# SSM group norms from column sums added on GpSimd, the skip product on ScalarE, another tile order, and no products for absent states

## The reference

```
zxbcdt = rms_norm(x, ln_g) @ in_w                 # z 2048, x 2048, B 512, C 512, dt 32 columns
xbc = silu(causal_dwconv(xbc, conv_w, conv_b))    # 4 taps; z is not convolved
dt = softplus(dt + dt_bias); a = dt * (-exp(a_log))
y = ssd_chunked(xs * dt, a, bm, cm)               # 4 chunks of 128 tokens, 4 groups of 8 heads
y = y + xs * d_skip[:, None]                      # the skip product
y = y.reshape(b, s, D_INNER) * silu(z)
y = rms_norm(y.reshape(b, s, 4, 512), norm_g)     # one norm for each group and token
return y @ out_w
# in ssd_chunked, for chunk c of group g:
#   y_diag = (C B^T, causal, times exp(decay)) x ; y_off = C state * exp(cumsum a) ; state = state * decay + B^T (decay x)
# the state before chunk 0 is zero
```

## Time and profile before

| what | us |
|---|---|
| time before, median of 3 runs | 2184.73 (2184.66 to 2185.71) |
| time of the profiled execution | 2181.98 |
| its span, first to last instruction | 2180.2 |
| PE busy in the span | 2117.6 (97%) |
| DVE busy | 1438.2 (66%) |
| ACT busy | 922.2 (42%) |
| POOL busy | 37.5 (2%) |

### The profile page before, as it was taken

How to read it: one execution, slowest core, us unless ns; L and a number is a source line. 1 busy time by engine, 2 the same in 40 slices (tenths; PEclk the granted TensorE clock), 3 DMA queues, 4 the chain that set the end, 5 groups by cost and what they waited for, 6 DMA issues and landing times.

```text
span 2180.2 us, 26967 instructions
## 1 busy us (share of the span) xinstructions
PE 2117.6 (97%) x10340; PEld 1677.1 (77%) x10340; DVE 1438.2 (66%) x2089; ACT 922.2 (42%) x1522; POOL 37.5 (2%) x100
## 2 busy tenths in 40 slices
PE   9999998899999999999899999999999999999998
PEld 7777776788888887777678888787777777767686
DVE  6687898777777345656577777447577657455664
ACT  5565655334444224444454444224343232344531
POOL 0000000000000000111000000000000000000000
PEclk9999999999999999999999999999999999999999
DMA  4321221222222333111132222333222224111132
GB/s 171 110 68 59 68 68 41 66 97 96 96 97 83 96 100 117 59 59 49 34 102 96 97 96 83 97 95 98 78 78 68 72 73 155 49 41 47 44 111 77
DMA packets 55072, 179.46 MB, mean 82 GB/s; under 512 B 6159, under 2 KB 7311, under 8 KB 54840
## 3 DMA queue, kind: packets, MB, share of 16 engines
q1 hardware_dynamic: 51264, 167.79, 23.8%
q10 hardware_dynamic: 3704, 10.30, 1.4%
HBM read 175.95 MB, written 4.74 MB: 83 GB/s over the span
## 4 chain that ended last, share of the span: by engine, by line
PE 76%; DVE 3%; ACT 1%; issue 0%; DMA 0%; DVEq 0%; ACTq 0%
PE bankpair L286 22%; PE bankpair L290 21%; PE bankpair L287 21%; PE bankpair L1445 1%; PE bankpair L699 1%; PE bankpair L1478 1%; PE bankpair L1459 1%; PE bankpair L719 1%; PE bankpair L1294 1%; PE bankpair L1306 1%; PE bankpair L709 1%; PE bankpair L664 1%; PE bankpair L1308 0%; PE bankpair L1392 0%; PE bankpair L674 0%
## 5 line engine op out<-in xcount | busy, mean ns | idle before, releaser
L286 PE MATMUL bankpair<-scaled_in_high,weights_high 128*128 128x512 f32 x1856 | 748.8, 403 | 5.0 <-DVE padded_rows L1747 2.2
L287 PE MATMUL bankpair<-scaled_in_low,weights_high 128*128 128x512 f32 x1856 | 728.0, 392 | 0.0
L310 ACT ACTIVATE weights_high<-weight_ring 128x1024 fp32r<-128x1024 f32 (+3 forms) x344 | 334.0, 972 | 314.1 <-DMA weight_ring<-down_dram 155.2
L290 PE MATMUL bankpair<-scaled_in_high,weights_low 128*128 128x512 f32 x1856 | 465.1, 389 | 0.0
L286 PEld LDWEIGHTS bankpair<-scaled_in_high,weights_high 128*128 128x128 f32 x1856 | 350.9, 189 | 89.9 <-issue 7.1
L321 DVE TENSOR_TENSOR weights_low<-weight_ring,weights_high 128x1024 fp32r<-128x1024 f32 (+3 forms) x344 | 383.8, 1125 | 54.5 <-ACT weights_high L310 45.0
L287 PEld LDWEIGHTS bankpair<-scaled_in_low,weights_high 128*128 128x128 f32 x1856 | 351.0, 189 | 76.4 <-issue 5.7
L290 PEld LDWEIGHTS bankpair<-scaled_in_high,weights_low 128*128 128x128 f32 x1856 | 348.6, 188 | 72.8
L286 PE MATMUL bankpair<-gated_high,weights_high 128*128 128x512 f32 x448 | 178.3, 398 | 4.6 <-DVE gated_low L2362 3.9
L287 PE MATMUL bankpair<-gated_low,weights_high 128*128 128x512 f32 x384 | 152.3, 397 | 0.0
L561 DVE SCALAR_TENSOR_TENSOR conv_rows<-padded_rows,params,conv_rows 128x512 f32<-128x512 f32 x176 | 131.8, 749 | 7.0 <-ACT conv_rows L530 3.8
(11 more groups left out here) (363 smaller groups left out, 2462.6 us busy)
## 6 DMA issues: line engine op xcount, KB each, us to landing
weight_ring<-up_dram SPq DMA_DIRECT2D x88, 512.0 KB, 3.6
weight_ring<-w_in_dram SPq DMA_DIRECT2D x70, 512.0 KB, 3.7
weight_ring<-in_w_dram SPq DMA_DIRECT2D x40, 512.0 KB, 3.7
weight_ring<-down_dram SPq DMA_DIRECT2D x32, 384.0 KB, 3.0
weight_ring<-kvq_dram SPq DMA_DIRECT2D x24, 512.0 KB, 3.7
weight_ring<-down_dram SPq DMA_DIRECT2D x32, 320.0 KB, 2.9
weight_ring<-out_a_dram SPq DMA_DIRECT2D x8, 512.0 KB, 3.7
weight_ring<-out_b_dram SPq DMA_DIRECT2D x8, 512.0 KB, 3.6
```

The source lines that it names most:

```text
L286: nc.tensor.matmul(bank, WH[:, high_slot, cell], high, start=(k == 0), stop=False)
L287: nc.tensor.matmul(bank, WH[:, high_slot, cell], low, start=False, stop=False)
L290: mm = nc.tensor.matmul(bank, WL[:, slot, cell], high, start=False, stop=(c == last_k))
L310: nc.scalar.activation(WH[:, (PART0[name] + k) % SLOTS, 0:n], RAW[:, b % SLOTS, 0:n], ACT.Copy).then_inc(high_ready, 1)
```

## The change

The mixer is rewritten in these places:

- Tile order within a group: B, C, x, z, where it was z, x, B, C. `FILL` becomes 2, 2, 3, 3. So chunk 0 is filled with B and C of the next group, chunk 1 with two tiles of x, chunk 2 with two of x and one of z, chunk 3 with three of z.
- Sums of squares: GpSimd adds the four squares of a unit to one (two instructions), and PE makes one product of it with a column of ones, which leaves a column of 128 sums. Root and reciprocal are taken of 128x4 elements, and PE spreads the four columns over the partitions with four transposes (`spread_root`) into bank 5. `group_norm` reads bank 5 and runs in chunk 3 of the next group (chunk 2 in the last group), after that unit's first tile.
- Since the sums of chunk 0 would overwrite a column that ACT has yet to read, PE waits for `gstd_ready` (ACT's root of the group before) ahead of the head of chunk 1 in groups 1 to 3.
- The skip product moves from DVE (one 128x512 instruction) to ACT (four of 128x128).
- In chunk 0, where the state is absent, ACT's `ECS` exponentials and DVE's two instructions on them are left out.
- One `split_low` in each unit comes before the wait for the exponentials.
- `ZS` is waited for by DVE's gating instead of by PE's head. The first `DTC` step on DVE comes ahead of `rows(0, 0)`.
- Three semaphores of the last norm of the program become one, with the same waits.

```diff
+        NORM_AT = {1: 3, 2: 3, 3: 2}
+        def exps_before(u):
+            return u - (u + NT - 1) // NT
+        def norms_before(u):
+            return sum(NT * g + NORM_AT[g] < u for g in NORM_AT)
+        def xb_row(j):
+            return GT + j if j < 2 else j - 2
-        FILL = [3, 2, 3, 2]
+        FILL = [2, 2, 3, 3]
+        CONVS = GT + 2
...
             def unit_sums(u):
-                pe.wait_ge(gsq_ready, u + 1)
-                for k in range(GT):
-                    mm = nc.tensor.matmul(BANK[4][:, 2 * P:3 * P], ONES[:, :], YSQ[:, k, :], start=(k == 0), stop=(k == GT - 1))
-                mm.then_inc(usum_done, 1)
+                pe.wait_ge(sq_added, 2 * u + 2)
+                at = 2 * P + u % NT
+                nc.tensor.matmul(BANK[4][:, at:at + 1], YSQ[:, 0, :], ONES[:, 0:1], start=True, stop=True).then_inc(usum_done, 1)
+
+            def spread_root(g, u):
+                pe.wait_ge(d_ready, u + 1)
+                pe.wait_ge(ginv_ready, g + 1)
+                for c in range(NT):
+                    mm = nc.tensor.transpose(BANK[5][:, c * P:(c + 1) * P], GINV[:, c:c + 1].to_broadcast([P, P]), IDENT)
+                mm.then_inc(gspread, 1)
...
                     if u >= 1:
                         pe.wait_ge(d_ready, u)
-                        pe.wait_ge(e_ready, 2 * u)
-                    if u >= 2:
-                        pe.wait_ge(gs_read, u - 1)
+                        pe.wait_ge(b_ready, u)
+                    if exps_before(u):
+                        pe.wait_ge(e_ready, exps_before(u))
+                    if c == 1 and g:
+                        pe.wait_ge(gstd_ready, g)
+                    if norms_before(u):
+                        pe.wait_ge(yn_ready, GT * norms_before(u))
...
-                            pe.wait_ge(row_used, GROUP_TILES * g + GT + j + 1)
+                            pe.wait_ge(row_used, GROUP_TILES * g + 2 + j + 1)
                         nc.tensor.transpose(BANK[5][:, j * P:(j + 1) * P], xb[:, j, tok], IDENT)
-                    if c == 0:
-                        pe.wait_ge(row_used, GROUP_TILES * (g + 1))
...
                             in_tile(g + 1, j)
+                            if g >= 1 and c == NORM_AT[g] and j == sum(FILL[:c]):
+                                spread_root(g - 1, u)
...
             for cells in (range(0, GT), range(GT, 2 * GT)):
                 for j in range(2):
                     gemm_tile(pe, "out_b", 0, j, lambda k: y_parts(k, j == 0), cells)
+                    if j == 0 and cells[0] == 0:
+                        spread_root(SSM_G - 1, UNITS - 1)
...
             def group_rms(g):
-                act.wait_ge(gs_read, NT * (g + 1))
-                nc.scalar.activation(STD[:, :], GSS, ACT.Sqrt, bias=EPSC[:, 0:1], scale=1.0 / (GT * P)).then_inc(gstd_ready, 1)
+                act.wait_ge(usum_done, NT * (g + 1))
+                if g:
+                    act.wait_ge(ginv_ready, g)
+                nc.scalar.activation(GROOT, BANK[4][:, 2 * P:2 * P + NT], ACT.Sqrt, bias=EPSC[:, 0:1],
+                                     scale=1.0 / (GT * P)).then_inc(gstd_ready, 1)
...
+                    for j in range(GT):
+                        skip = nc.scalar.activation(TMPY[:, j, :], XSB[g % 2][:, j, c * P:(c + 1) * P], ACT.Identity,
+                                                    scale=par("ssm_d", GT * g + j))
+                    skip.then_inc(skip_ready, 1)
...
                     act.wait_ge(yb_ready, u + 1)
+                    if u:
+                        act.wait_ge(usum_done, u)
                     nc.scalar.activation(YSQ, YB[:, GT * g:GT * (g + 1), c * P:(c + 1) * P], ACT.Square).then_inc(gsq_ready, 1)
                     if c == 0 and g >= 1:
                         group_rms(g - 1)
                         exp_tables(ahead)
-            square_sums(UNITS - 1)
+            nc.scalar.preload_act_table_set("sqrt_and_others")
             group_rms(SSM_G - 1)
...
+            for u in range(UNITS):
+                pool.wait_ge(gsq_ready, u + 1)
+                if u:
+                    pool.wait_ge(usum_done, u)
+                nc.gpsimd.tensor_tensor(YSQ[:, 0:2, :], YSQ[:, 0:2, :], YSQ[:, 2:4, :], ALU.add).then_inc(sq_added, 1)
+                pool.wait_ge(sq_added, 2 * u + 1)
+                nc.gpsimd.tensor_tensor(YSQ[:, 0, :], YSQ[:, 0, :], YSQ[:, 1, :], ALU.add).then_inc(sq_added, 1)
...
             def group_norm(g):
-                dve.wait_ge(gstd_ready, g + 1)
-                rs.step(nc.vector.reciprocal(RSG[:, :], STD[:, :]))
+                dve.wait_ge(gspread, g + 1)
...
-                    step.step(nc.vector.tensor_copy(etot, ecs[:, :, P - 1]))
-                    step.step(nc.vector.tensor_tensor(ecs, ecs, xb[:, GT + 1, tok].unsqueeze(1).to_broadcast([P, SSM_HG, P]),
-                                                      ALU.mult))
+                    if c:
+                        step.step(nc.vector.tensor_copy(etot, ecs[:, :, P - 1]))
+                        step.step(nc.vector.tensor_tensor(ecs, ecs, xb[:, GT + 1, tok].unsqueeze(1).to_broadcast([P, SSM_HG, P]),
+                                                          ALU.mult))
+                    if g + 1 < SSM_G:
+                        split_low(dve, BASE["in_w"] + GROUP_TILES * (g + 1) + sum(FILL[:c]) + 2)
...
-                    step.step(nc.vector.tensor_tensor(TMPY, xb[:, 0:GT, tok],
-                                                      par("ssm_d", GT * g, GT).unsqueeze(2).to_broadcast([P, GT, P]), ALU.mult))
+                    dve.wait_ge(skip_ready, u + 1)
                     dve.wait_ge(y_done, u + 1)
                     yr.step(nc.vector.tensor_tensor(TMPY, TMPY, BANK[6][:, :].rearrange("p (j t) -> p j t", t=P), ALU.add))
+                    if c == 0:
+                        dve.wait_ge(row_used, GROUP_TILES * (g + 1))
...
-                    if c == 0 and g >= 1:
-                        group_norm(g - 1)
+                    if c == 1 and g >= 1:
+                        group_inverse(g - 1)
```

94 lines of the change are left out of this document (53 added, 41 removed).

## The result

The changed kernel takes **2160.64 us** (median; 2157.72 to 2162.02 in 4 runs), the kernel before, in the same rounds, 2184.69 us (2182.45 to 2185.71). The ratio is **0.9892, 95% interval 0.988 to 0.9904**: 24 us faster. Forecast were 2165, between 2152 and 2177. The profiled execution took 2160.4 us with a span of 2158.6, against 2181.98 and 2180.2: 21.6 us less.

What follows compares the result with a forecast made beforehand. PE, busy 97% of the span, was taken as the bound, so only its work, waits or clock could give time. The terms summed to -19.5 us from 2181.98; with the median's 2.7 us offset, 2165 was forecast, range 2152 to 2177.

Steps and rivals of the forecast that it cites:

- Sums: On PE, sixteen sums of squares fall from four products to one single-column product each: gain 11.7 us.
- Spreads: On PE, four spreads of four transposes each are added: loss 1.8 us.
- Start: PE's wait at the mixer's start falls from 4.4 to about 1.9 us and the clock stays up: gain 4.0 us.
- Heads of chunk 0: PE's waits there for Silu of tile C and for the copied sum go: gain 11.0 us.
- operands after the norm: PE's waits behind the long reciprocal and four scalings go, with the low clock behind them: gain 18.1 us together.
- The new wait: PE's head of chunk 1, groups 1 to 3, waits for ACT's root, then low clock: loss 23.0 us.
- DVE behind in group 0: DVE starts chunk 2 some 5 us late, so a z tile waits for its bank: loss 3.0 us.
- Skip product: Moved from DVE to ACT, which has room for 1.2 us more a unit: no cost of its own.
- Entry to `out_a`: Waits for the first tiles' low parts fall from 1.8 to about 1.3 us: gain 0.5 us.
- End of the mixer: Waits and low clock around the last norm fall from 7.9 to 5.9 us: gain 2.0 us.
- The new wait was not cheap: Rival for chunk 1's head: clock holds or soon recovers, table loads early; 8.0 + 3.8 us more saved, 2153; chance 0.17.
- Contention of DVE and GpSimd: Rival: GpSimd's additions stop DVE, which becomes the bound; 12.5 us, up to 2177.5; chance 0.13.

Runs made afterwards that it cites:

- the early eviction: On the kernel with the later root, DVE empties a unit's first bank ahead of `split_low` and the decay's products in chunks 1 to 3: 2134.8 us.
- the kernel with the later root: The changed kernel with ACT's root moved one chunk later, behind the skip products, and PE waiting for it only before the next sum: 2148.68 us.

## Why the prediction was right, point by point

The profiled execution became 21.6 us shorter; the sum said 19.5.

- **Sums.** -11.7 forecast. The trace shows 0.99 - 0.20, sixteen times, -12.6. The size held. But as an edit it is worth less: in the experiment with the sums on PE 4.7 of the 10.6 us added vanished in waits. The price of work on PE is its length only where no wait stands behind it.
- **Spreads.** +1.8, as forecast: one inside a unit takes 0.60 us for four transposes, of which some 0.45 are before the next product starts.
- **Start.** -4.0 forecast. The wait is 1.96 us (1.9 said), the head starts 1.96 us earlier, and the clock stays whole, where the earlier trace rows had 4.0 us at half. The wait was foreseen; that the clock held was in part luck. Behind the same 1.96 us wait it fell in seven of the eleven kernels that have it, for some 3.4 us, which costs 1.7.
- **Heads of chunk 0** and **operands after the norm.** -29.1 forecast. None of these waits is left, nor a window of low clock at their places. The experiment with the old order brings 10.2 and 5.8 us of them back and is 16.7 us slower. What the shorter reciprocal and the later place of the scalings give by themselves was not tried. One term was missed: the prediction read no low clock behind the waits of 2.5 us. Behind the third of them, in group 3, the trace of before has it. PE there, from the end of the wait:

```profile
332.12 0.33 PE L2126 MATMUL bankpair<-constants,arena 128*128 128x128 f32 x1 [2.47 <-ACT arena L2213]
...
334.32 0.63 PE L286 MATMUL bankpair<-scaled_in_high,weights_high 128*128 128x512 f32 x1
334.75 0.63 PE L287 MATMUL bankpair<-scaled_in_low,weights_high 128*128 128x512 f32 x1
```

  The products start 0.43 us apart, where they do so every 0.23 us at the full clock; from 333.5 to 337.2 us the granted clock is 0.54 in the mean. That is another 1.7 us, which the change took away.
- **The new wait.** 5.8, 5.8, 3.4 forecast; 5.92, 6.03, 3.68 measured, through the chain that was named. The clock: 8.0 forecast; by length and level of the three windows 4.2 x 0.45 + 5.2 x 0.50 + 4.2 x 0.41 = 6.2, and filling the waits gave 6.9. Together 21.8 for 23.0.
- **DVE behind in group 0.** One bank wait, 3.0 forecast, 2.65 measured, in the chunk that was named, and DVE is 5.9 us behind there (5 said). What the step left out is the clock behind it, 4.0 x 0.43 = 1.7 us. It also named only DVE's work as the cause; the early eviction removed the wait with the same work, by its order alone.
- **Skip product.** Forecast without a cost or a gain of its own; undoing it costs 3.2 us by the medians.
- **Entry to `out_a`.** 1.8 became 0.9: -0.9 for -0.5.
- **End of the mixer.** -2.0 forecast, and the step was too hopeful: 3.57 + 1.2 us of waits and half of 5.8 at low clock, 7.7 for 5.9; -0.2. The chain of adding, gating, square and additions needs 3.6 and not 3.1 us, as GpSimd takes 754 and 488 ns for 128x256 and 128x128, not my 520 and 260 by halving 1.04.

With the measured terms the sum is -12.6 + 1.8 - 4.0 - 29.1 + 21.8 + 4.4 - 0.9 - 0.2 = -18.8, and -20.5 with the missed 1.7 us. By the starts of the heads it is group 3 where the first sum falls short, by some 2 us, which fits. Of the 1.1 us left to the measured -21.6, the part behind the mixer holds 0.5. So the total came out as close as it did partly because misses cancel: the sums, the clock behind the root's waits and the missed window against the clock behind the bank wait and the end of the mixer.

The rivals. The new wait was not cheap: neither did the clock hold nor was the table loaded early, though both can be had, for 8.0 and 3.0 us by the medians. Contention of DVE and GpSimd exists and hardly touches this change. The clock recovered within 4 to 6 us, so it did not stay low. DVE was not behind in every unit so that PE waited: with the wait for the root in place, only group 0 has a bank wait of more than 0.2 us.

The prediction had said that the new wait lets DVE catch up, so that a bank wait is not paid twice. The experiments give this a size: the root's wait and its clock are 21.8 us, but removing them alone gives 12.0, since bank waits take their place, and with the bank waits gone too it is 25.8.

## What to carry to other kernels

A wait that gives another engine time to catch up is worth less than its length: before removing it, look which wait of that engine's comes next, and remove both. Where a bank's reader is late, first ask what stands ahead of that one instruction on its engine; here an order within DVE was worth more than any of the work taken off it. Price idle time on PE with what the clock loses behind it: in these kernels 1.3 to 3.4 us behind each wait of 3.15 us and more, and mostly 1.7 us behind 18 of the 30 waits of 2 to 3 us. Where idle products fill a wait, make them end before it does.

## What the runs showed of the hardware

- PE's clock behind its waits, counted in the mixer of all thirteen profiles. Behind the 12 waits of 1.1 to 1.6 us it was whole for the next 3 us each time. Around or within 1.1 us of the end of each of the 42 waits of 3.15 us and more it was at 1.2 GHz. The 30 waits of 1.96 to 3.01 us have both: 18 with a stretch at 1.2 GHz in the 3 us behind them, 12 without, and a wait of the same length can do either. Waits of 2.65 to 2.67 us in group 0 were followed by it in three kernels and not in two; one of 3.01 us had none. Two stretches in the kernel with the later root, behind a wait of 1.96 us at the start and behind one of 2.35 us in group 1:

```profile
78.30:82.00 3.70, 3.69 (x18) 3.50 (x19) 0.99 (x3) 0.85 (x2) 0.00 (x0) 0.60 0.31 97
203.00:207.00 4.00, 4.00 (x18) 3.29 (x19) 2.98 (x5) 3.67 (x5) 0.00 (x0) 1.00 0.10 41
```

  So one profile doesn't tell what the clock does behind a wait of 2 to 3 us; what it depends on stays open here.
- How long it stays low varies for the same wait: 5.8 us after the 3.57 us wait in the changed kernel, 2.7 us after the same 3.57 us in the kernel that evicts early.
- Idle products kept the clock up: 24 of 128x128 took 5.5 us, at no cost where PE would have waited longer than that. At the end of the mixer 14 of them took 3.2 us and outlasted what PE waited for by 0.95 us.
- GpSimd's additions get shorter by less than their size: 1041 ns for 128x512, 754 for 128x256, 488 for 128x128.
- A DVE instruction on two SBUF operands took 1.95 instead of 1.23 us beside GpSimd's additions; one with an operand in a bank took 1.23 beside them.
- A one-column product of a 128x128 operand takes 0.21 us, four in a row 0.87; four with 128 columns took 0.99. One column in place of 128 saves little; one product in place of four does.
